# The last pair of a projection woven into the attention heads that follow it

## The reference, cut to what matters

```
layer 0:  x -> norm -> projection "even" (mLSTM and stick-breaking heads) -> mixer -> "out0" -> + x -> norm -> MLP 0 -> + x
layer 1:  x -> norm -> projection "odd"  (q, k, v, r, g_down)             -> GLA   -> "out1" -> + x -> norm -> MLP 1 -> + x

GLA, per head h of 4 (key width 128, value width 256), per chunk, decay log_g = log_sigmoid(g_down @ w_gate_up + b) / 16:
  b     = cumsum(log_g)
  o     = (q * exp(b)) @ S + A @ v,     A[t,s] = sum_k q k exp(b_t - b_s) for s <= t
  S_new = exp(b_last) * S + (k * exp(b_last - b))^T @ v
out:  y = rms_head(o) * g_head * silu(r);   mix = y @ w_out
```

## Time and profile before

| what | value |
|---|---|
| median of the runs shown | 1729.4 us (the lowest 1729.17) |
| profiled execution | 1730.9 us, span 1729.1 us |
| PE matmul busy | 1615.4 us, 93% of the span |
| DVE, ACT, POOL busy | 881.9 (51%), 593.2 (34%), 91.8 us (5%) |
| chain that ended last | PE 81%, DVE 8%, ACT 4%, issue 3%, DMA 2% |
| mean granted clock of TensorE | 0.959 |

### The profile page before, as it was taken

How to read it: one execution, slowest core, us unless ns; L and a number is a source line. 1 busy time by engine, 2 the same in 40 slices (tenths; PEclk the granted TensorE clock), 3 DMA queues, 4 the chain that set the end, 5 groups by cost and what they waited for, 6 DMA issues and landing times.

```text
span 1729.1 us, 31543 instructions
## 1 busy us (share of the span) xinstructions
PE 1615.4 (93%) x12446; PEld 1450.4 (84%) x12446; DVE 881.9 (51%) x1563; ACT 593.2 (34%) x946; POOL 91.8 (5%) x168
## 2 busy tenths in 40 slices
PE   6899998999989999999999798987699999999996
PEld 6899985444479999999999788975499999999995
DVE  4544554546627544444446646655528354444445
ACT  4223233454435322332225433333236222223324
POOL 0000001324400000000000000000000000000000
PEclk9999999999989999999999898987699999999998
DMA  4312118889752222212222111232112222222221
GB/s 171 123 59 89 61 61 298 292 324 358 267 187 92 75 74 96 97 73 74 96 97 82 64 62 50 75 134 86 61 50 74 74 98 81 70 91 97 73 74 54
DMA packets 50522, 195.14 MB, mean 113 GB/s; under 512 B 7325, under 2 KB 9534, under 8 KB 36610
## 3 DMA queue, kind: packets, MB, share of 16 engines
q1 hardware_dynamic: 35938, 139.49, 22.7%
q0 software_dynamic: 14496, 54.41, 8.4%
HBM read 182.19 MB, written 11.68 MB: 112 GB/s over the span
## 4 chain that ended last, share of the span: by engine, by line
PE 81%; DVE 8%; ACT 4%; issue 3%; DMA 2%; SPq 2%; POOLq 0%; POOL 0%; DVEq 0%; ACTq 0%
PE ps L309 22%; PE ps L311 21%; PE ps L310 21%; DMA kbuf<-in_k_cache_dram 2%; PE ps L1313 2%; ACT whi L294 2%; DVE wlo L298 1%; SPq L1292 1%; PE ps L1340 1%; PE ps L1548 1%; PE ps L1506 1%; PE ps L2091 1%; PE ps L2083 1%; PE ps L1452 1%; PE ps L2092 1%
## 5 line engine op out<-in xcount | busy, mean ns | idle before, releaser
L309 PE MATMUL ps<-xhi,whi 128*128 128x280 f32 x2112 | 627.8, 297 | 30.2 <-DVE wlo L298 17.5
L311 PE MATMUL ps<-xhi,wlo 128*128 128x280 f32 x2112 | 620.7, 294 | 0.0
L310 PE MATMUL ps<-xlo,whi 128*128 128x280 f32 x2112 | 619.9, 294 | 0.0
L309 PEld LDWEIGHTS ps<-xhi,whi 128*128 128x128 f32 x2112 | 403.2, 191 | 37.8 <-DVE wlo L298 19.4
L310 PEld LDWEIGHTS ps<-xlo,whi 128*128 128x128 f32 x2112 | 402.8, 191 | 0.5
L311 PEld LDWEIGHTS ps<-xhi,wlo 128*128 128x128 f32 x2112 | 402.7, 191 | 0.0
L298 DVE TENSOR_TENSOR wlo<-raw,whi 128x2048 fp32r<-128x2048 f32 x98 | 224.5, 2291 | 212.0 <-ACT whi L294 211.4
L294 ACT ACTIVATE whi<-raw 128x2048 fp32r<-128x2048 f32 x97 | 185.4, 1912 | 403.1 <-PE ps L311 402.2
L309 PE MATMUL ps<-dhi,whi 128*128 128x280 f32 x1024 | 300.6, 294 | 5.4 <-DVE wlo L298 4.9
L311 PE MATMUL ps<-dhi,wlo 128*128 128x280 f32 x1024 | 300.2, 293 | 0.0
L310 PE MATMUL ps<-dlo,whi 128*128 128x280 f32 x1024 | 299.3, 292 | 0.0
(11 more groups left out here) (403 smaller groups left out, 1460.9 us busy)
## 6 DMA issues: line engine op xcount, KB each, us to landing
raw<-in_weights_dram SPq DMA_DIRECT2D x98, 1024.0 KB, 4.8
kbuf<-in_k_cache_dram SPq DMA_DIRECT2D x128, 256.0 KB, 5.2
vbuf<-in_v_cache_dram POOLq DMA_DIRECT2D x128, 256.0 KB, 8.2
s0b<-in_gla_in_dram POOLq DMA_DIRECT2D x4, 1024.0 KB, 5.1
out_dram<-s0b POOLq DMA_DIRECT2D x4, 1024.0 KB, 4.6
hT<-in_x_dram SPq DMA_DIRECT2D x2, 1120.0 KB, 8.2
out_dram<-pj POOLq DMA_DIRECT2D x2, 1120.0 KB, 8.6
hT<-in_x_dram POOLq DMA_DIRECT2D x2, 1120.0 KB, 13.4
```

What stands on the lines that cost most here:

```text
L309: pe.matmul(out, whi[:, par, t, :], hi, start=first, stop=False)
L310: pe.matmul(out, whi[:, par, t, :], lo, start=False, stop=False)
L311: return pe.matmul(out, wlo[:, par, t, :], hi, start=False, stop=last)
```

## The change

The last pair of the odd projection (the gate rows of heads 2 and 3) is no longer done by `pair4_pe`. Its eight outputs become pieces of 24 matmuls each, all in PSUM bank 6 and each evicted by DVE (`piece_pe`, `piece_dve`). Pieces 0 and 1 stand around the turn of head 0. In heads 0, 1 and 2 one piece stands ahead of the output products (out) and one ahead of the transposes back. What the new `gla_pe` orders for a head is chunks, meta (the meta tokens' product, now in a bank half of its own), samples, last, piece, out, turn of the next head, piece, back, with the meta and sample tokens' value transposes of the next head (`gla_turn4_pe`) inside back.

For this `xhi`, `xlo`, `whi`, `wlo` stay in place through the heads, and the heads' buffers move: VT, KT, KVk into slot 1 of `raw`, single instead of double; Ss, sfin, gqm, KVv, sr to other places; two PSUM bank pairs (GKS) alternate between heads. Hence out1's first slab is loaded once slot 0 is split, its second when the last head's outputs are done. ACT scales two of the five normed outputs of a head (DVE did all five). The steps that lay under pair 5 move: last_q, last_sub and their exponentials under pair 4, pick 7, last_k and compose_act to the start of the heads. Levels 0 and 1 go from after outputs (2,4) and (2,6) to after (2,6) and (3,0); a memset of ATd moves from the scan to (2,5). The states are stored per head.

The mix of out1 is split in three parts (heads 0 and 1; 2; 3), the first during head 3, and PE waits for them by block. At the start of the program slab 0 is split in eight strips that alternate with the blocks of `xhi` and `xlo`, PE waits by strip, and SP loads both slabs ahead of the second half of x.

The core of the diff (the functions that only move their buffers are left out):

```diff
             for h in range(2):
                 for par in range(2):
-                    if h == 0:
+                    if h == 0 and (par or name != "even"):
                         pe.wait_ge(S["lo"], SLAB0[name] + par + 3)
                     if wait_bank:
                         wait_bank(4 * h + 2 * par + 1)
...
                 pe.wait_ge(S["x_lo"], 16 * NORM[name] + 8 * h + k + 1)
+                if name == "even" and h == 0:
+                    if k < KB - 1:
+                        pe.wait_ge(S["w_lo"], k + 1)
+                    else:
+                        pe.wait_ge(S["lo"], 3)
             return wait_k
 
         def pair4_pe(pe, i, name, beside):
...
             act.wait_ge(XLD[0], 16)
-            x_hi_act(act, "even", 0, 0, 0, range(KB))
-            split_hi(act, 0, 0)
+            for k in range(KB):
+                x_hi_act(act, "even", 0, 0, 0, (k,))
+                if k == 0:
+                    act.wait_ge(RAW[0], 16)
+                act.activation(whi[:, 0, k::KB, :], raw[:, 0, k::KB, :], ACT.Copy).then_inc(S["hi" if k == KB - 1 else "w_hi"], 1)
+            split_hi(act, 0, 1)
             x_squares_act(act, 0)
-            split_hi(act, 0, 1)
             act.wait_ge(XLD[1], 16)
...
             dve.wait_ge(XLD[0], 16)
-            x_lo_dve(dve, "even", 0, 0, 0)
-            split_lo(dve, 0, 0)
+            for k in range(KB):
+                x_lo_dve(dve, "even", 0, 0, 0, (k,))
+                if k < KB - 1:
+                    dve.wait_ge(S["w_hi"], k + 1)
+                else:
+                    dve.wait_ge(S["hi"], 1)
+                dve.tensor_tensor(wlo[:, 0, k::KB, :], raw[:, 0, k::KB, :], whi[:, 0, k::KB, :].bitcast(f32), ALU.subtract)\
+                   .then_inc(S["lo" if k == KB - 1 else "w_lo"], 1)
             split_lo(dve, 0, 1)
             x_tree_dve(dve, "even", 0)
...
+                if name == "out0":
+                    if k % 4 == 0:
+                        pe.wait_ge(S["mx_lo"], 2 * h + k // 4 + 1)
+                elif k in (0, 4, 6):
+                    pe.wait_ge(S["mx_lo"], 2 * POST[name] + 2 * max(0, k // 2 - 1) + h + 1)
             first_pair_pe(pe, name, wait_k, lambda n: None)
...
-        LEVEL_PE = {(2, 4): 0, (2, 6): 1, (3, 3): 2, (3, 5): 3, (4, 0): 4, (4, 3): 5, (4, 5): 6, (4, 7): 7}
+        LEVEL_PE = {(2, 6): 0, (3, 0): 1, (3, 3): 2, (3, 5): 3, (4, 0): 4, (4, 3): 5, (4, 5): 6, (4, 7): 7}
...
             elif at_ == (2, 4):
                 level_x(dve, 1)
+            elif at_ == (2, 5):
+                own.link(dve.memset(ATd[:, :, :], 0.0))
...
                 level_pick(dve, 6)
-            elif at_ == (5, 0):
-                level_pick(dve, 7)
                 last_q(dve)
-            elif at_ == (5, 1):
+            elif at_ == (4, 7):
                 last_sub(dve)
-            elif at_ == (5, 3):
-                last_k(dve)
 
...
-            elif at_ == (2, 7):
+            elif at_ == (3, 1):
...
-            elif at_ == (5, 0):
+            elif at_ == (4, 5):
...
-            elif at_ == (5, 2):
+            elif at_ == (4, 7):
                 act.wait_ge(S["g_ex"], 8)
                 act.activation(E[:, :, :], E[:, :, :], ACT.Exp, scale=1.0 / TAU).then_inc(S["g_E"], 1)
-            elif at_ == (5, 4):
-                compose_act(act)
...
+        def piece_pe(pe, j, ks):
+
+            par, f, h = j // 4, j % 4 // 2, j % 2
+            if ks[0] == 0:
+                pe.wait_ge(S["lo"], LAST * 2 + SLAB0["odd"] + par + 3)
+                pe.wait_ge(S["ev"], EV["odd"] + 8 * LAST + j)
+            for k in ks:
+                mm = product(pe, ps[:, 6, 0:HALF], par, f * KB + k, xhi[:, k, COLS[h]], xlo[:, k, COLS[h]],
+                             k == 0, k == KB - 1)
+            if ks[-1] == KB - 1:
+                mm.then_inc(S["done"], 1)
+
+        def piece_dve(dve, j):
+            par, f, h = j // 4, j % 4 // 2, j % 2
+            dve.wait_ge(S["done"], DONE["odd"] + 8 * LAST + j + 1)
+            dve.tensor_tensor(pj[:, 4 * LAST + 2 * par + f, COLS[h]], ps[:, 6, 0:HALF], r_in[:, h], ALU.mult)\
+               .then_inc(S["ev"], 1)
 
...
+            pe.wait_ge(S["h_y"], 2 * h + 2)
+            for b in range(2):
+                mm = pe.transpose(ps[:, 3, P * b:P * (b + 1)], on4[:, b * P:(b + 1) * P], ident)
+            mm.then_inc(S["h_yt"], 1)
             if h + 1 < H_C:
-                pe.wait_ge(S["h_kv"], h + 2)
+                gla_turn4_pe(pe, h + 1)
             for b in range(2):
                 for c in range(4):
-                    pe.transpose(ps[:, 4 + b, c * P:(c + 1) * P], on[:, c, b * P:(b + 1) * P], ident)
+                    mm = pe.transpose(ps[:, GKS[h % 2][b], c * P:(c + 1) * P], on[:, c, b * P:(b + 1) * P], ident)
+            mm.then_inc(S["h_yt"], 1)
+
+        def gla_pe(pe):
+            pe.wait_ge(S["g_c"], 5)
+            piece_pe(pe, 0, range(KB))
+            gla_turn_pe(pe, 0)
+            gla_turn4_pe(pe, 0)
+            piece_pe(pe, 1, range(KB))
+            for h in range(H_C):
+                gla_chunks_pe(pe, h)
+                gla_meta_pe(pe, h)
+                gla_samples_pe(pe, h)
+                gla_last_pe(pe, h)
+                if h < 3:
+                    piece_pe(pe, 2 + 2 * h, range(KB))
+                gla_out_pe(pe, h)
+                if h < 3:
+                    gla_turn_pe(pe, h + 1)
+                    piece_pe(pe, 3 + 2 * h, range(KB))
+                gla_back_pe(pe, h)
...
+                act.wait_ge(S["h_rs"], h + 1)
+                for c in range(2):
+                    ins = act.activation(on[:, c, :], gla_out_bank(h, c), ACT.Copy, scale=grs[:, c:c + 1])
+                ins.then_inc(S["h_y"], 1)
                 if h + 1 < H_C:
                     gla_values_act(act, h + 1)
                     gla_gate_act(act, h + 1)
+                if h == 1:
+                    act.wait_ge(S["done"], DONE["odd"] + 8 * LAST + 4)
+                    split_hi(act, SLAB0["out1"] // 2, 0)
+                if h == 2:
+                    act.wait_ge(S["done"], DONE["out1"])
+                    act.wait_ge(S["h_mix"], 3)
+                    for half in range(2):
+                        gla_mix_hi(act, 0, 4, half)
...
+        def gla_scan_dve(dve, h):
             u = h % 2
+            dve.wait_ge(S["h_kv0"], h + 1)
             if h == 0:
+                dve.wait_ge(S["h_at"], 10)
+            copy = dve.tensor_copy(Ss[:, 0, :], ps[:, 3, DV_C:2 * DV_C])
+            copy.then_inc(S["h_c0"], 1)
+            dve.wait_ge(S["h_c0"], h + 1)
+            for c in range(4):
+                add = ps[:, GKS[u][c // 2], (c % 2) * DV_C:(c % 2 + 1) * DV_C]
...
+                elif c == 2:
+                    ins.then_inc(S["h_S"], 1)
+                    dve.wait_ge(S["h_S"], h + 1)
+                else:
+                    ins.then_inc(S["h_sf"], 1)
+
+        def gla_carry_dve(dve, h):
...
+            dve.wait_ge(S["h_kvs"], h + 1)
+            dve.wait_ge(S["h_t4"], h + 1)
...
+            ins.then_inc(S["h_s0"], 1)
...
         def gla_dve(dve):
-            dve.wait_ge(S["done"], DONE["out1"])
+            level_pick(dve, 7)
+            last_k(dve)
             dve.wait_ge(S["g_el"], 3)
+            piece_dve(dve, 0)
+            dve.wait_ge(S["g_fin"], 2)
+            dve.wait_ge(S["g_z"], 2)
             gla_keys_dve(dve, 0)
+            gla_last_dve(dve, 0)
+            piece_dve(dve, 1)
             for h in range(H_C):
+                gla_scan_dve(dve, h)
+                if h < 3:
+                    piece_dve(dve, 2 + 2 * h)
+                gla_carry_dve(dve, h)
+                if h == 2:
+                    split_lo(dve, SLAB0["out1"] // 2, 0)
+                if h == 3:
+                    for half in range(2):
+                        gla_mix_lo(dve, 0, 4, half)
+                rr = pj[:, RC + 2 * h:RC + 2 * h + 2, :]
+                dve.wait_ge(S["h_sg"], h + 1)
+                dve.tensor_tensor(rr, sr[:, :, :], rr, ALU.mult).then_inc(S["h_sr"], 1)
+                dve.wait_ge(S["h_rs"], h + 1)
+                for c in (4, 2, 3):
+                    ins = dve.tensor_scalar(on[:, c, :] if c < 4 else on4[:, :], gla_out_bank(h, c), grs[:, c:c + 1], None,
+                                            ALU.mult)
+                ins.then_inc(S["h_y"], 1)
+                if h < 3:
                     gla_keys_dve(dve, h + 1)
+                    gla_last_dve(dve, h + 1)
+                gla_tail_dve(dve, h)
+                if h < 3:
+                    piece_dve(dve, 3 + 2 * h)
+                gla_mix_dve(dve, h)
+            for k in (4, 6):
+                for half in range(2):
+                    gla_mix_lo(dve, k, 2, half)
+            split_lo(dve, SLAB0["out1"] // 2, 1)
...
             sp_.dma_start(gn[:, :, :, :], gains).then_inc(S["gld"], 16)
+            sp_.dma_start(hT[:, :, COLS[0]], x[:, :, COLS[0]]).then_inc(XLD[0], 16)
             for h in range(2):
```

(31 more changed lines are left out.)

276 lines of the change are left out of this document (144 added, 132 removed).

## The result

The changed kernel takes **1683.5 us** (median of 1676.5 to 1686.0); the kernel before, in the same series, 1729.3 (one of its four executions took 2286.6 us; the ratio leaves it out). The ratio is 0.974 with an interval of 0.970 to 0.978: faster, by 2.6%. The forecast was 1688, range 1678 to 1702. Two later repeats of the same kernel gave medians of 1681.9 (ratio 0.972, 0.968 to 0.975) and 1682.4 (0.972, 0.969 to 0.975).

What follows compares the result with a forecast made beforehand. The prediction took the GLA stage to be bound by a chain of short steps on three engines, with PE idle and at low clock. Gains of 36.4 + 2.5 + 3.1 = 42 us gave 1688 us, range 1678 to 1702.

Steps and rivals of the forecast that it cites:

- What bounds the kernel: Whole kernel: PE busy nearly throughout; GLA stage a chain of short steps on three engines, PE idle 6 to 9 us a head.
- The GLA term: From level 7's end to out1's first matmul: 134.0 us before, 97.6 us after, a gain of 36.4 us.
- Front: From level 7's end to the start of the heads: PE stands about 9 us, the front ends after 22.1 us.
- three heads: Heads 0 to 2: PE's work at full clock 19.35 us a head plus 0.15 for waits, 58.5 us together.
- Head 3: Last head, nothing woven: PE waits about 5 us for the norm; out1's first matmul 17.0 us after the head's start.
- Odd pairs 2 to 4: Odd projection: the 6.7 us wait for level 0 goes, about 5 us stop at pair 3 instead; gain 2.5 us (0 to 5).
- The start: Program start: PE begins after one block and one strip, about 10 to 11.5 us; gain 2 to 4, taken as 3.1 us.
- The sum: Whole kernel: 36.4 + 2.5 + 3.1 = 42 us off the profiled execution's 1730.9 us.
- The heads at 1.2 GHz: GLA heads: PE's clock falls during small products and transposes; price 24 us, 1712, half of it 1700; chance 0.15.
- DVE's order sets the head: Heads: an eviction holds up the carry, so the turn comes late; 2 to 3 us in three heads, 1694 to 1698; chance 0.12.
- The small parts give nothing: Start and odd pairs gain nothing, or PE stops once more with half clock behind it: 1692 to 1698; chance 0.08.
- The woven outputs hide nothing: Heads stay bound by the chain through ACT and DVE: 1731.5, or 1737 if the small parts fail; chance 0.03.

Runs made afterwards that it cites:

- thin pieces: Changed kernel with pieces 2 to 7 cut from 24 matmuls to 3 (one block row of eight): 1669.9 us.
- front experiment: Changed kernel with pick 7, piece 0's eviction and last_k ahead of the last slab's low part, piece 1 ahead of turn 0, head 0's values within the composition: 1677.1 us.
- both undone parts: Two runs against the changed kernel: the program's start as before, 1686.3 us; levels 0 and 1, ATd's clearing and the copy to ATo put back, 1688.5 us.

## Why the prediction was right, and where its terms were off

- **What bounds the kernel.** Right: the GLA stage was a chain at low clock, and the woven products filled it. The thin pieces show it from the other side: take PE's work out, and the period falls with it. No run takes back ACT's share of the normed outputs or the states stored per head by themselves; what these are worth isn't shown.
- **The GLA term, 36.4 us forecast, 42.1 measured** (134.15 -> 92.03). Front 20 us (22.1 forecast), three heads 56.4 (58.5), head 3 15.7 (17.0). The mechanism was that of the text, the sizes were each a little too long. In the heads, the sum of PE's work, 19.35, counted the turn and the transposes back to the end of their last matmul, where the next group has already begun: from start to start turn and back together took 3.60 us (4.25 in the sum), samples to chunks 5.03 (5.3), the outputs 3.62 (3.6), the woven outputs 6.35 (6.2). That makes 18.6, the busy time of PE. The allowance of 0.15 us for waits is 0.22 measured, all of it for the carry, which the text has some 0.2 us late. The front's stop is 9.8 us by the text's own sum (12.9 less 3.1) and "about 9" in its words; it was 8.4, by the very queue that the text counted: the last key product behind a low part that waits for ACT. What was too long in that sum is its first term: DVE was 1.0 us behind at pair 4's last output, not 1.9. The front experiment shows the price of that order: 8 us.
- **Head 3.** The norm wait "about 5 us" was 4.65. The load of out1's second slab, taken as 0, cost 0.
- **Odd pairs 2 to 4, forecast 2.5 (0 to 5).** Measured 4.7 in the profiled execution, 6 against the repeats, when put back. The step was right in both halves, the 6.7 us wait gone and "about 5 us" at pair 3 in its place (4.70). What was mis-sized is what remains: the text counted only pair 2's queued outputs; but level 4's stop fell from 2.0 to 0.8 us as well, and level 0's products ran at full clock, 2.1 us instead of 3.6. The text had no term for either.
- **The start, forecast 3.1.** 4.1 us at the first matmul, 3.8 at the gates (40 us); at 92 us 2.2 to 2.4 in eight of the eleven executions, 3.7 to 3.8 in two, 0.7 in one. The path was right: PE passed to the second slab at 19.75 us instead of 23.62, once its low part was there. ACT took 0.73 us a block, not 0.83, so this gain is larger than 3.1. The text let it run through to the end; in nine of the eleven a stretch at half clock before 92 us takes 1.5 us of it (in one of these two such stretches). In the profiled execution three more stretches at half clock cost 4.7 us, so that the start seems to give nothing at all there; the repeats show that these come and go with the execution.
- **The sum.** 42 forecast, 44.9 in the profiled executions, and that it comes so near is in part luck, for the errors have both signs: +5.7 in GLA, +2.2 in the odd pairs, -0.9 at the start, and -4.7 in the mLSTM heads, for which the text has no term. (0.5 us come back between 240 and 1008 us.)
- **The rivals.** *The heads at 1.2 GHz*: refuted, 1.00 in all three, through some 6 us of small products and transposes in each. By the Trainium skill (TensorE: Matmul & The Clock Gate, Part 4, PE-mode transpose) transposes do not bring PE to its full clock; here they stand between full products, and the clock of 1.00 is held. No run here has transposes alone. With small products among them the clock even rose: of the ten executions that stop 8.4 us ahead of head 0's turn, six come back to full clock within that turn, before any product of 128x280 (in the first repeat 0.50 from 1126.22 to 1127.00 us, 0.91 in the next 0.90 us). *DVE's order sets the head*: not in heads 0 to 2; the carry keeps PE for 0.22 us. Head 2 has the least slack, 2.4 us by the thin pieces. *The small parts give nothing*: refuted by the traces of both undone parts, 2.2 to 3.9 us at 92 us and 4.7 to 6 us at level 7's end. *The woven outputs hide nothing*: refuted; the heads with two outputs in them take 18.8 us, less than the 24 to 26 us that they took without any. Its sum has a slip that changes nothing: 18.5, 98.5, 2.6 and 22.1 make 141.7, not 143.2, so its price is 1730 and not 1731.5.

## What to carry to other kernels

Where a chain of short steps over three engines alternates with long matmuls that don't depend on it, weave them in whole outputs: the gain is the chain's idle time and the clock that it cost, and the forecast is PE's sum of work at full clock as long as the chain without the woven work is shorter. Then read the new queue order for work that stands in front of what the next engine waits for, above all where it itself waits for a third engine: here three such places were worth 14 us, beside the 46 to 51 us of the change. For gains of a few us, compare stages between traces rather than medians, and repeat the execution before giving a half-clock stretch a cause.

## What the runs showed of the hardware

The granted clock fell to 0.50 in the mLSTM heads with PE busy without a gap, in a run of small transposes and products, and it did so in three heads of one execution, none of the next and three of the third, with the same code: 1.58 us each time. A wait of 2.8 us ahead of the last transposes back left the clock at 0.99 over the stretch; with one of 4.65 us it was 0.90. Behind a stop of 8.4 us the clock rose in six of ten executions while PE did transposes and small products only, in four of them later. And PE stood 0.5 to 1.0 us (nine executions) or 2.0 to 2.2 us (four) in the midst of level 4, and went on each time 1.3 to 1.5 us after a packet on the instruction queue had landed.
